# Rounding and splitting weight groups three groups ahead of their multiplication in place of two, in a four-layer float32 kernel

## The reference

```python
# first block, each of 2 layers
mod = silu(c) @ w_mod + b_mod                       # 2048 x 6144 per layer
shift, scale, gate = split(mod, 3)
h = rms_norm(x, g_pre) * (1 + scale) + shift
proj = h @ w_in                                     # 2048 x 5648
y = concat(window_attention, spatial_gating, gated_linear_attention)(proj) * silu(z)
x = x + gate * rms_norm(y @ w_out, g_post)          # 2048 x 2048
# second block, each of 2 layers
proj = rms_norm(x) @ w_in                           # 2048 x 3648
x = x + concat(mla, differential, chunk_band attention)(proj) @ w_o
x = x + square(relu(rms_norm(x) @ w_up)) @ w_down   # 2048 x 8192 and 8192 x 2048
```

## Time and profile before

| | |
|---|---|
| median of 3 runs | 2894.59 us (2892.93 to 2895.9) |
| the profiled execution's own time | 2896.87 us |
| its span | 2893.4 us |
| granted TensorE clock, mean | 0.994 |
| instructions | 37180 |
| moved by DMA | 611.89 MB, mean 211 GB/s |

### The profile page before, as it was taken

The page is one execution under the profiler, slowest core; times in us unless marked ns, Lnnn a source line. Parts: engine busy times, 40 slices in busy tenths (PEclk is TensorE's granted clock), DMA queues, the critical chain, the costliest instruction groups (busy, mean ns, idle before and its releaser), DMA issues.

```text
span 2893.4 us, 37180 instructions
## 1 busy us (share of the span) xinstructions
PE 2808.0 (97%) x14535; PEld 2424.4 (84%) x14535; DVE 2071.0 (72%) x2672; ACT 1487.4 (51%) x2079; POOL 41.8 (1%) x48
## 2 busy tenths in 40 slices
PE   5998998999999999999999999999999999999998
PEld 5886787898889888888888888898888888888887
DVE  7998998779855567666666677745666666666774
ACT  4445544665546555644444455565556444444443
POOL 0000000000000000000000000000000000000000
PEclk9999999999999999999999999999999999999999
DMA  9996598867755555555665556555545555555563
GB/s 388 366 354 226 191 350 305 279 190 261 246 172 174 162 171 163 178 189 192 196 197 188 189 196 200 186 179 156 174 163 174 189 196 197 197 187 189 199 211 138
DMA packets 173885, 611.89 MB, mean 211 GB/s; under 512 B 19680, under 2 KB 19952, under 8 KB 173072
## 3 DMA queue, kind: packets, MB, share of 16 engines
q1 hardware_dynamic: 170912, 600.42, 60.8%
q0 software_dynamic: 1824, 6.61, 0.8%
q10 hardware_dynamic: 976, 2.51, 0.2%
HBM read 607.34 MB, written 2.11 MB: 211 GB/s over the span
## 4 chain that ended last, share of the span: by engine, by line
PE 86%; DVE 7%; ACT 3%; DMA 2%; issue 1%; SPq 0%; POOL 0%; POOLq 0%; ACTq 0%; DVEq 0%
PE ps L2198 17%; PE ps L2201 17%; PE ps L2205 17%; PE ps L2265 16%; PE ps L2275 8%; DVE w_lo L1347 2%; PE ps L2140 2%; DVE raw L1575 2%; PE ps L2475 1%; PE ps L2244 1%; PE ps L2242 1%; PE ps L2239 1%; ACT w_hi L946 1%; PE ps L2454 1%; PE ps L2253 1%
## 5 line engine op out<-in xcount | busy, mean ns | idle before, releaser
L1347 DVE TENSOR_TENSOR w_lo<-raw,w_hi 128x1024 fp32r<-128x1024 f32 (+4 forms) x988 | 1145.8, 1175 | 655.2 <-ACT w_hi L946 651.7
L946 ACT ACTIVATE w_hi<-raw 128x1024 fp32r<-128x1024 f32 (+4 forms) x988 | 992.5, 1018 | 1104.5 <-PE ps L2205 501.0
L2198 PE MATMUL ps<-w_hi,hT_both 128*128 128x512 f32 (+3 forms) x1824 | 479.0, 384 | 17.1 <-DVE proj L1547 8.1
L2265 PE MATMUL ps<-hT_both,w_hi 128*128 128x512 f32 x2048 | 490.2, 391 | 0.9 <-DVE u L1503 0.9
L2201 PE MATMUL ps<-w_lo,hT_both 128*128 128x512 f32 (+3 forms) x1824 | 462.1, 375 | 0.6 <-DVE w_lo L1347 0.6
L2205 PE MATMUL ps<-w_hi,hT_both 128*128 128x512 f32 (+3 forms) x1824 | 459.4, 373 | 0.0
L2265 PEld LDWEIGHTS ps<-hT_both,w_hi 128*128 128x128 f32 x2048 | 376.2, 188 | 74.1 <-DVE u L1503 1.3
L2201 PEld LDWEIGHTS ps<-w_lo,hT_both 128*128 128x128 f32 x1824 | 339.8, 189 | 50.6 <-DVE w_lo L1347 1.9
L2198 PEld LDWEIGHTS ps<-w_hi,hT_both 128*128 128x128 f32 x1824 | 327.1, 189 | 64.4 <-DVE proj L1547 11.9
L2205 PEld LDWEIGHTS ps<-w_hi,hT_both 128*128 128x128 f32 x1824 | 339.0, 188 | 48.1
L2275 PEld LDWEIGHTS ps<-hT_both,w_lo 128*128 128x128 f32 x2048 | 262.8, 191 | 10.2
(11 more groups left out here) (298 smaller groups left out, 2082.5 us busy)
## 6 DMA issues: line engine op xcount, KB each, us to landing
raw<-in_w_up SPq DMA_DIRECT2D x256, 512.0 KB, 3.6
raw<-in_w_down SPq DMA_DIRECT2D x256, 512.0 KB, 3.5
raw<-in_w_modT SPq DMA_DIRECT2D x192, 512.0 KB, 5.7
raw<-in_w_rest SPq DMA_DIRECT2D x80, 456.0 KB, 3.4
raw<-in_w_z SPq DMA_DIRECT2D x64, 512.0 KB, 4.5
raw<-in_w_out SPq DMA_DIRECT2D x64, 512.0 KB, 4.4
raw<-in_w_rest SPq DMA_DIRECT2D x48, 344.0 KB, 3.5
raw<-in_w_oa SPq DMA_DIRECT2D x32, 512.0 KB, 3.4
```

The lines of the kernel that those rows point to most:

```text
L946: act.activation(hi_blocks(L % SPLIT_SLOTS, c, w), blocks(raw, G % RAW_SLOTS, c, w), ACT.Copy).then_inc(S.hi_ready, 1)
L1347: dve.tensor_tensor(blocks(w_lo, r, c, w), blocks(raw, r, c, w), hi_blocks(s, c, w).bitcast(F32), ALU.subtract).then_inc(S.group_read, 1)
L2198: pe.matmul(o, rows(hi, c, t), wh[:, c], start=start and c == 0, stop=False)
L2265: pe.matmul(ps[:, bank(job, i, f)], wh[:, c, f * P:(f + 1) * P], hT_both[:, k0 + c].rearrange("p a n -> p (a n)"), start=k0 + c == 0, stop ...
```

## The change

One constant goes from 2 to 3, and both places that read it follow.

```diff
--- before.py
+++ after.py
@@ -39,7 +39,7 @@
 RAW_SLOTS = 10
 SPLIT_SLOTS = 4
-AHEAD = 2
+AHEAD = 3
 TAIL = 4
```

## The result

The changed kernel takes 3014.61 us (median; 3011.99 to 3019.13) against 2894.56 us: a ratio of 1.0414, 95% interval 1.0401 to 1.0427, 120 us more. The direction was as forecast, the size twice the forecast, and outside the range of 2922 to 2980 us.

A forecast was written before the change was run, and what follows sets the result against it. PE, busy 97% of the span, was taken as the bound, so its added waits cost in full. Terms summed to +63.8 us, taken as +60 on the median of 2894.59: 2955 us, range 2922 to 2980.

The forecast's parts named there:

- the six steps between down tiles: From one pair of down tiles to the next: readout behind the next group's split, +1.67 us each, +10.0 us.
- the first up tiles: First tile of an up product, twice: a rounding and a split come ahead of u's copy, +3.3 us.
- the tail of out1: ACT's squares stand behind a rounding, so x is updated later: +3.3 us (1 to 4).
- the ends of up products: Four places: u's last copy behind a held rounding, then combine and split before its readout: +4.1 us each, +16.5.
- the first 300 us: Later mod loads and readouts: ina0 to ind0 7.5 us (0 to 15), z0 7 (0 to 14); together +14.5.
- the loop through the loads: Rival, ina0 to z0: late loads delay PE, which releases later loads; 43 us in place of 14.5, 2984 us; chance 0.16.
- the rows of PE keep their means: Sign of being right: apart from the named growing waits, PE's rows keep their mean times.
- in1: From 470 to 530 us: five activation chunks wait behind a later group's rounding and its load, +13 us (5 to 20).
- uqr, ukn and uv: Second block's short tiles: readouts delayed behind a rounding at two places per layer, 0.75 us each, +3.0 (0 to 4).
- only the first 530 us suffer: Rival: later readouts have slack, so only the early terms cost; about 2921 us, chance 0.12.
- The relief of PE by earlier splits: Rival: three ready groups let PE absorb late loads or late DVE, at most 13 us gained; 2882 us, chance 0.04.
- it is hidden: Rival: the change stays within 0.2%, 2889 to 2900 us; chance 0.04.

The follow-up runs named there:

- e1: Changed kernel (three ahead), with readouts placed ahead of each step's rounding and splitting of weights on ACT and DVE: 2967.23 us, ratio 1.0256.
- e6: Changed kernel (three ahead) with five slots for rounded groups instead of four and nine load slots instead of ten: 3012.25 us, ratio 1.0409.
- e9: Changed kernel (three ahead) with z0's 28 mods spread evenly over its 32 steps: 2996.29 us, ratio 1.0344.
- e5: As e1, with activations' rounding and splitting and the attention and gating steps also ahead of a step's weights; its output differs in parts: 2922.42 us, ratio 1.0096.
- e10: Control for e9: the kernel before (two ahead) with z0's mods spread evenly: 2898.96 us, ratio 1.0008.
- e13: Changed kernel (three ahead) with readouts and activations first, z0's mods spread evenly, and readouts of ina0 to ind0 one step earlier: 2914.73 us, ratio 1.0075.
- e11: As e1, with activations' rounding and splitting also ahead of a step's weights, attention steps left where they were: 2947.77 us, ratio 1.0180.
- e3: Kernel before (two ahead, its ACT queue kept), with loads and DVE's reading of mods in the changed kernel's order: 2920.94 us, ratio 1.0095.
- e8: Kernel before (two ahead) with the readouts ahead of each step's rounding and splitting, as in e1: 2891.98 us, ratio 0.9991.
- e12: Kernel before (two ahead) with readouts and activations' rounding and splitting ahead of a step's weights, as in e11: 2891.64 us, ratio 0.9982.
- e4: Kernel before (two ahead) with 2, 3, 4 and 6 idle DVE operations ahead of the last u readout at the four ends of up products: 2909.29 us.

## Why the prediction was right or wrong

**What was right.** Hardly any wait was for weights, and the gain was the 1.3 us of waits that vanished. The mechanism (a readout behind a rounding that PE holds one group longer) is shown by e1 and e6, one of which moves the readout and the other frees the slot. Behind 530 us, where the sum rested on rows, most of it held: the six steps between down tiles at 1.5 us each (9.0, forecast 10.0), the first up tiles 3.4 (3.3), the tail of out1 3.8 (3.3), the idle time at the ends of up products 4.64 each (4.1).

**The step that failed first: the first 300 us, "+14.5 (0 to 29)".** They measured 41.2 (15.5 and 25.7). For z0 I priced "1 us on each of the 14 steps with mods", as if only the issue of a load moved. The change takes a step's distance from both ends: the load is released as late as before and is asked for one step earlier, and its landing (3.2 to 8.3 us from 230 to 330 us, median 4.9) then stood at the head of ACT's queue, with the attention's copies behind it. e9 shows the landing and e5 the queue; either alone removes all but a few us of it (4.4 left in e9 against e10, none in e5, which also drops waits). For ina0 to ind0 e13 shows that the loss is the readout behind the split, the mechanism of my other terms, which I had put at "half a split" on 24 tiles: with the loads in the changed kernel's order 12.7 us were lost in e11 and none in e13, which moves these readouts. The loads that were to share the blame had no part that shows, though with two ahead they cost 3.7 us there (e3). The rival of the loop through the loads had this stretch at 43 us, and it should have had a larger chance than 0.16. That it came so close to 41.2 is partly luck: a load that lands late and holds up what follows is the cause in z0 alone, which is 25.7 of it, and its whole time, 2984 us, is 31 short.

**The second: the price of a stall.** Each term was the idle time of PE alone. I had expected that the rows of PE keep their means. Over the whole trace 41.5 of the 121 us are matmuls that take longer, most of it (some 37 us) at the lower clock. At the ends of up products it makes 6.7 to 7.3 us out of 4.64, 27.9 in all in place of 16.5. The row on z0 of before had a clock of 0.90 beside 13.3 us of idle time, and I read it and didn't use it.

**Smaller ones.** in1 was 20.5 (13, within its 5 to 20 but for half a us); uqr, ukn and uv 3.2 for layer 0 and 3.2 for layer 1 (3.0 for both), because PE lost time at four places per layer and not at two; 2.8 us in each of the attention stretches of the second block and 2.7 from 330 to 470 us, which I hadn't listed. The range was also drawn too tight: the bounds of the single terms add up to some 2926 to 2980 us and not to 2935 to 2973.

**The rivals.** That only the first 530 us suffer is refuted by 58.5 us after them. The relief of PE by earlier splits isn't seen in any stretch. That it is hidden is refuted by the 120 us.

By terms: 26.7 us of the miss of 57 are the first 330 us, 11.4 the ends of the up products, 7.5 in1, and the rest the small stretches. Right terms for the first 300 us alone would have given about 2982 us, still 33 short: the clock and the small terms are needed as well.

## What to carry to other kernels

Preparing work further ahead adds no work (DVE and ACT were as busy as before), but on an engine that works through its queue in order it puts a wait in front of everything that the engine does for others. Before raising a lookahead, list what stands behind the prepared step on its engine, and find what releases that step: if it is the consumer's last group, or a load that is itself released by it, the readouts inherit the wait. A cheaper question than how far ahead is whether the readout can stand first; here that removed all but 8.3 of the 58.5 us behind 530 us, and gained the shorter lookahead some 0.1 to 0.2%. Two controls belong to it: the same move without the longer lookahead (e8, e12), and a trace of a stretch that nothing touches, which tells how far two executions differ anyway (up to 6 us in z0).

Price a stall of TensorE by its length and then look at the granted clock in the windows behind it. Here stalls of 3.4 to 5.1 us at the ends of up products cost 1.6 to 2.9 us more than they lasted. Shorter ones (1.96 and 2.68) cost what they lasted there, but one of 2.12 us cost 1.6 us more in e9 than one of 2.11 in the changed kernel, so a short stall isn't safe.

## What the runs showed of the hardware that was not expected

The granted clock was 0.50 right behind a stall of 5.1 us in a stretch in which PE was busy for 4.00 of 4.00 us before (window 1429:1433). The first four matmuls behind it took 2.08 us and the next four 1.91, in place of 1.20 and 1.07, and the price hardly follows the length: 1.6 us for one of 4.86 (e4), 1.6 to 2.9 for four of 3.40 (e6), 2.1 to 2.6 for four of 5.14.

Nor does the length say whether the clock falls. It stayed at 1.00 behind stalls of 2.68 us (e4), 2.11 (the changed kernel, first tile of up00) and 3.65 (e1, tail of out1), and it fell behind one of 1.96 at 110 us of the changed kernel (four matmuls of 0.98 us took 1.75), one of 2.12 and one of 3.65 (both e9). What decides it, no run here shows.
